# A one-core decoder layer with 32 experts: three gate_up widths, an order of the experts worked out on the chip, and changed stage openings

## The chip, the core and the metric

The kernel runs on one core of a Trainium2 chip. The metric is the device time of one launch in microseconds. The kernel before was timed three times: median 2191.45 us, from 2190.69 to 2195.38. Lower is better. The core has five engines with programs of their own, which meet only at semaphores: TensorE (PE, with its weight loads listed as PEld), VectorE (DVE), ScalarE (ACT), GpSimd (POOL) and SyncE (SP, which only issues DMAs here).

## The reference

One layer over x of 1024 tokens by 1024 features, all float32:

- h = RMSNorm(x); one projection h @ W_in of 3584 columns. 2048 of them feed four retention heads (rotary, chunks of 128, decay, norm, gate), 1536 feed eight stick-breaking attention heads of 64.
- x = x + concat(retention, attention) @ W_out.
- x = x + MoE(RMSNorm(x)): a router picks the top 4 of 32 experts per token with softmax weights over the four logits.

The mixture of experts, cut to its core:

```
top_logits, top_idx = lax.top_k(xf @ w_router + b_router, 4)
top_w = softmax(top_logits)
for each expert e, for its tokens xb:
    gu     = xb @ w_gate_up[e] + b_gate_up[e]      # 1024 -> 2048
    gate   = min(gu[:, 0::2], 7);  up = clip(gu[:, 1::2], -7, 7)
    hidden = (up + 1) * gate * sigmoid(1.702 * gate)
    y      = hidden @ w_down[e] + b_down[e]        # 1024 -> 1024
    out[token] += y * weight
```

There are 4096 assignments of a token to an expert, 128 per expert in the mean. Gate and up columns alternate in w_gate_up. An expert's weights are 12.6 MB.

## The kernel before

**Stages ahead of the experts (0 to 647 us).** Each tile of 128 tokens is normalised and transposed (`turn_tile`). The input projection goes in two halves of 512 tokens, 28 slabs of weights in all. Each float32 operand is split into an upper part (fp32r) by ACT and the rest by DVE (`upper_tokens`, `lower_tokens` and their like for slabs), and three products are summed (L946, L953). Of the first half's four tiles, DVE normalises 0 and 1 and POOL 2 and 3 (L592). Retention runs beside the projection. Then come the stick-breaking attention (393 to 508 us), the output projection (L1103 to L1105), the second norm and the router. Attention uses the difference `dv` of the values `sv` and the values shifted by one token: SP issues the shift as DMAs when the whole projection is done, POOL subtracts (L613).

**From the router to the first expert.** DVE picks the four best experts of each tile (`best`), PE ranks the tokens per expert (L1147, L1151), and DVE builds one-hot rows (`first_hot`), from which PE makes the list of expert 0's tokens. POOL gathers these rows from DRAM (`xn_scratch`, L616), PE transposes them (`turn_main`, `turn_over`), and DVE writes them as `xT`. Then `tables` on DVE (L1665 to L1679) builds the weights and places of all tokens, before the counters that PE waits for are raised (L1684). `keep_busy` is a row of transposes whose results nobody reads.

**The loop.** Every expert is one block, in the order 0 to 31, in a loop on all engines. In a block PE does:

- gate_up (L1246): 8 steps `f`, each 16 matmuls of 128x128 weights from `gu_ring` against w columns of `xT`. The weights of one matmul are every second column of a 256 wide piece (gate, then up). A branch on the expert's token count takes the program of w = 140 or w = 168, the most that a block holds. Step f writes PSUM bank f%2, which DVE must have emptied (`m_up`). After f = 3 comes `token_list` for the next expert (L1162).
- down (L1226): 48 matmuls for each half of the output with split operands; the next tokens' transposes lie inside. Tokens 129 to 160 go through `down_over(0)` and 161 to 168 through `down_over(1)`, 64 matmuls each (L1234), under a branch.

DVE adds biases, clips and multiplies per step, works out the next list (`list_hot` in f = 1, L1637 its first instruction, L1644 its largest; `list_out` in f = 4), and makes the lower parts of w_down. In block 0 it also does `table_part`, tables for experts over 168 tokens, which don't occur with these inputs. ACT does the sigmoid and the upper parts. SP asks for the next expert's weights as each quarter of `gu_ring` and the halves of `dn_ring` come free. POOL gathers the next tokens and adds this block's rows to the output in DRAM.

Semaphores count up over the whole run, and waits in the loop are on n times a constant. Nothing is planned at run time but the two branches.

## Time and profile before

One profiled execution took 2190.32 us, and its span, first to last instruction, is 2188.0 us.

| | |
|---|---|
| PE busy | 2126.4 us, 97% of the span |
| PE weight loads busy | 1891.9 us |
| DVE busy | 1271.9 us, 58% |
| ACT busy | 765.9 us, 35% |
| POOL busy | 346.5 us, 16% |
| chain of waits | PE 95%, DVE 2%, issue 1%, DMA 1% |
| moved by DMA | 509.53 MB |

Busy time is the union of an engine's instructions; weight loads lie beside matmuls. The chain of waits is followed back from the last instruction, at each step to what released it. "issue" is time in which an engine waited for nothing that the profile shows. A window's row gives the busy time of each engine in a stretch with the number of instructions in brackets, then the mean clock of PE as a share of full speed (PEclk), the DMA engines' share and their GB/s. A bare number such as 128x140 is the output of one instruction. L946 is line 946.

### The profile page before, as it was taken

Reading aid. Unit: us, or ns where it says so; the run is one execution under the profiler, and the core shown is the slowest. Engines: PE = TensorE matmul, PEld = TensorE weight load, DVE = VectorE, ACT = ScalarE, POOL = GpSimd, SP = SyncE. Lnnn points to the kernel's source line nnn. Section 1 sums busy time; section 2 is a strip of 40 time slices with the busy share of each in tenths; the row PEclk is TensorE's granted clock in tenths of the full one; section 3 lists DMA queues with packets and bytes.
Section 4 is the critical chain, followed back from the end, with each engine's and each line's share of the span. In section 5 each row is a group of like instructions: output and inputs, shape, how many; then the busy total and the mean of one; then the engine's idle time right before and its main releaser. Section 6 shows DMA issues by size and latency. Waiting matters only on the chain.

```text
span 2188.0 us, 41248 instructions
## 1 busy us (share of the span) xinstructions
PE 2126.4 (97%) x16059; PEld 1891.9 (86%) x16060; DVE 1271.9 (58%) x2564; ACT 765.9 (35%) x1369; POOL 346.5 (16%) x243
## 2 busy tenths in 40 slices
PE   7999999899979999999999999999999999999996
PEld 6887888677868999898899999899999999999996
DVE  6434534886466665456556655555666655666654
ACT  4143133666222333233333323333333332333332
POOL 3100200200011111111121111111212111212121
PEclk9999999999979999999999999999999999999998
DMA  5321221304366988788789888877998887999883
GB/s 179 105 79 58 97 96 39 116 1 154 126 209 220 323 307 293 238 279 307 274 298 318 306 293 280 307 270 263 320 325 307 306 294 264 319 327 331 309 290 89
DMA packets 253683, 509.53 MB, mean 233 GB/s; under 512 B 7466, under 2 KB 36318, under 8 KB 253342
## 3 DMA queue, kind: packets, MB, share of 16 engines
q1 hardware_dynamic: 230124, 451.95, 57.9%
q0 software_dynamic: 21968, 51.67, 9.6%
q10 hardware_dynamic: 1536, 5.15, 0.7%
q8 instruction: 38, 0.62, 0.1%
q14 instruction: 17, 0.14, 0.0%
HBM read 473.09 MB, written 33.55 MB: 232 GB/s over the span
## 4 chain that ended last, share of the span: by engine, by line
PE 95%; DVE 2%; issue 1%; DMA 1%; POOL 0%; ACT 0%; ACTq 0%; SPq 0%; DVEq 0%; POOLq 0%
PE bank L1246 46%; PE bank L1226 16%; PE bank L946 10%; PE bank L953 4%; PE bank L1234 3%; PE bank L1056 2%; PE bank L1069 2%; PE bank L1103 1%; PE bank L1169 1%; PE bank L1105 1%; PE bank L1104 1%; PE bank L1162 1%; PE bank L1040 1%; PE bank L1175 1%; PE bank L1211 1%
## 5 line engine op out<-in xcount | busy, mean ns | idle before, releaser
L1246 PE MATMUL bank<-hx,ring 128*128 128x140 f32 (+1 forms) x8192 | 1021.9, 287 | 7.5 <-DVEq L1684 7.5
L1246 PEld LDWEIGHTS bank<-hx,ring 128*128 128x128 f32 x8192 | 1015.1, 197 | 10.3 <-DVEq L1684 7.7
L1226 PE MATMUL bank<-work_r,hx_r 128*128 128x512 f32 x1024 | 335.0, 408 | 0.0
L1723 DVE TENSOR_TENSOR mix_r<-ring,work_r 128x1024 fp32r<-128x1024 f32 x256 | 305.0, 1223 | 41.1 <-ACT work_r L872 40.9
L889 ACT ACTIVATE hx<-hx 128x168 f32<-128x168 f32 x256 | 88.0, 344 | 595.8 <-DVE hx L1739 593.4
L1739 DVE TENSOR_SCALAR hx<-bank,small 128x168 f32<-128x168 f32 x256 | 100.3, 392 | 298.7 <-PE bank L1246 289.3
L872 ACT ACTIVATE work_r<-ring 128x1024 fp32r<-128x1024 f32 x256 | 257.7, 1042 | 0.0
L1226 PEld LDWEIGHTS bank<-work_r,hx_r 128*128 128x128 f32 x1024 | 188.1, 189 | 43.9 <-issue 10.4
L1226 PE MATMUL bank<-mix_r,hx_r 128*128 128x512 f32 x512 | 200.0, 391 | 0.0
L649 POOL DMA_INDIRECT out_x<-hx,small x32 | 52.0, 1625 | 659.7 <-ACT hx L882 621.3
L880 ACT ACTIVATE hx<-bank,small 128x512 f32<-128x512 f32 x64 | 44.0, 688 | 313.9 <-PE bank L1175 167.3
L616 POOL DMA_INDIRECT hx<-xn_scratch,small x33 | 33.9, 1028 | 574.1 <-issue 568.1
L895 ACT ACTIVATE hx_r<-hx 128x128 fp32r<-128x128 f32 x256 | 78.8, 308 | 109.0 <-DVE hx L1749 109.0
L946 PE MATMUL bank<-hx_r,mix_r 128*128 128x512 f32 x480 | 112.5, 392 | 3.6 <-DVE hx_r L1337 3.6
L1226 PEld LDWEIGHTS bank<-mix_r,hx_r 128*128 128x128 f32 x512 | 96.1, 188 | 21.0
L946 PE MATMUL bank<-hx_r,work_r 128*128 128x512 f32 x480 | 113.7, 394 | 0.0
L946 PEld LDWEIGHTS bank<-hx_r,mix_r 128*128 128x128 f32 x480 | 89.6, 188 | 23.5 <-issue 5.2
L1644 DVE TENSOR_TENSOR work<-hx,cst 128x3072 bf16<-128x3072 f32 x32 | 107.2, 3351 | 0.0
L946 PEld LDWEIGHTS bank<-hx_r,work_r 128*128 128x128 f32 x480 | 89.7, 188 | 20.2 <-issue 1.9
L652 POOL DMA_INDIRECT out_x<-hx,small x64 | 100.7, 1573 | 19.5 <-issue 19.5
L1741 DVE TENSOR_SCALAR hx<-bank,small 128x168 f32<-128x168 f32 x256 | 98.0, 383 | 0.0
L1658 DVE TENSOR_TENSOR hx<-bank,small 128x512 f32<-128x512 f32 x66 | 42.6, 686 | 86.0 <-PE bank L1169 86.0
(244 smaller groups left out, 2318.4 us busy)
## 6 DMA issues: line engine op xcount, KB each, us to landing
ring<-in_w_gate_up SPq DMA_DIRECT2D x128, 2048.0 KB, 11.0
ring<-in_w_down SPq DMA_DIRECT2D x64, 2048.0 KB, 17.5
mix<-in_w_in SPq DMA_DIRECT2D x14, 1024.0 KB, 5.0
work<-in_w_in SPq DMA_DIRECT2D x14, 1024.0 KB, 5.1
ring<-in_x SPq DMA_DIRECT2D x8, 512.0 KB, 6.3
hx<-in_w_out SPq DMA_DIRECT2D x1, 4096.0 KB, 14.0
work<-in_x ACTq DMA_DIRECT2D x8, 512.0 KB, 4.7
out_x<-work SPq DMA_DIRECT2D x8, 512.0 KB, 4.5
```

What stands on the lines that cost most here:

```text
L652: e.indirect_dma_start(out=out_quarters, in_=y_o[:, r], in_offset=None, compute_op=ALU.add, out_offset=bass.IndirectOffsetOnAxis(ap=idx_sc ...
L872: e.activation(dn_hi[:, nh, k:k + 2], dn_ring[:, k:k + 2, nh * CH:(nh + 1) * CH], ACT.Copy).then_inc(c_hi, 1)
L889: e.activation(sg[:, f % 2], g1[:, f % 2], ACT.Sigmoid, scale=GALPHA).then_inc(m_sig, 1)
L895: e.activation(hid_hi[:, f], hid[:, f, 0:P], ACT.Copy).then_inc(h_hi, 1)
L946: mm = e.matmul(dst, ws[b][:, k, u["s"] * P:(u["s"] + 1) * P], xs[:, k, :], start=k == 0 and (xs is x_hi and ws is w_hi), stop=k == KD - 1 ...
L953: mm = e.matmul(dst, xs[:, KD // 2 * b + k, u["s"] * P:(u["s"] + 1) * P], ws[b].rearrange("p (k a) n -> p k (a n)", a=2)[:, k, :], start=b ...
L1226: mm = e.matmul(bank[2 + t][:, :], h[:, k], w[:, t, k], start=False, stop=k == KD - 1 and w is dn_lo, skip_group_check=True)
L1246: mm = e.matmul(bank[f % 2][:, part * CAP:part * CAP + w], gu_ring[:, k, f * 256 + part:(f + 1) * 256:2], xT[:, k, 0:w], start=k == 0, sto ...
L1644: e.tensor_tensor(hot, pos_s.unsqueeze(2).to_broadcast([P, NT, NH * P]), slot_at.unsqueeze(1).to_broadcast([P, NT, NH * P]), ALU.is_equal) ...
L1723: e.tensor_tensor(dn_lo[:, nh, k:k + 2], dn_ring[:, k:k + 2, nh * CH:(nh + 1) * CH], dn_hi[:, nh, k:k + 2].bitcast(F32), ALU.subtract).the ...
L1739: e.tensor_scalar(g1[:, b], bank[b][:, 0:CAP], be[:, f:f + 1], GLIM, ALU.add, ALU.min)\
L1741: e.tensor_scalar(u1[:, b], bank[b][:, CAP:2 * CAP], be[:, 8 + f:9 + f], GLIM + 1.0, ALU.add, ALU.min).then_inc(m_up, 1)
```

## The change

1. *Widths and order.* There are three gate_up programs, 128, 140 and 168 columns wide (`WIDTHS`), chosen by two nested branches. Experts 0, 1 and 2 stay first (`FIXED`); of the others, those over 140 tokens (`LATER`) come last. The order is worked out on DVE during block 1 (`order_part`), so every engine that needs a block's expert (SP for its loads, DVE for its tables) reads it from `it_i` in memory. A new semaphore `it_go` says how many entries are ready; SP waits for it, and so does PE before its token count.
2. *Tables.* The opening's `tables` are split: the second expert's list (`second_lists`, `second_hot`) and the weights and places (`weight_table`, `place_table`) go into block 0, `order_part` into block 1 and `table_part` into block 2. ACT's split of b_down (`bias_part`) also moves into block 0.
3. *First tiles.* Tile 2 is normalised by ACT and tile 3 by DVE instead of POOL. PE does 14 idle transposes before the first vectors.
4. *Second token half.* Half of its split (`upper_tokens`, `lower_tokens`) is done before the last slab of the first half ends (g == NG // 2 - 3).
5. *Stick-breaking values.* `dv` is two regions; the first half's shift and subtraction are done within the projection.
6. *Output projection.* 20 idle transposes at its opening; `best` and `route_sum` of a tile are placed earlier in the loop over tiles.
7. *Experts' opening.* The rows of b_gate_up are loaded early into part of `dn_ring`, and their transposes stand earlier on PE; the second half of w_down waits for them. The last tile of normalised tokens is stored by ACT, not SP.

The diff, cut (only changed lines, indentation reduced):

```
@@ -58,9 +58,11 @@
-WIDTHS = (140, CAP)
-IT_STEPS = 17
-F_SPREAD = 20
+WIDTHS = (128, 140, CAP)
+LATER = (140,)
+FIXED = 3
+IT_STEPS = 28
+F_SPREAD = 21
...
-  b_rows = region(work, 4096, 2048)[0:NE]
+  b_rows = dn_ring[0:NE, 0:4, 512:1024]
...
@@ -530,6 +540,12 @@
+   def shifted(q):
+    lo = HT * q
+    for r0, r1 in ((1, 113), (113, P)):
+     e.dma_start(dv[q][r0:r1], sv[r0 - 1:r1 - 1, lo:lo + HT]).then_inc(z_shift[q], 16)
+    e.dma_start(dv[q][0:1, 1 - q:HT], sv[P - 1:P, lo - q:lo + HT - 1]).then_inc(z_shift[q], 16)
@@ -540,32 +556,35 @@
+    if j == NSLAB // 2 + 4:
+     e.wait_ge(prj_free, freed(NG // 2))
+     e.wait_ge(xs_lo, KD)
+     shifted(0)
-   for q in range(2):
-    lo, n = HT * q, HT - 1 + q
-    for r0, r1 in ((1, 113), (113, P)):
-     e.dma_start(dv[r0:r1, lo:lo + HT], sv[r0 - 1:r1 - 1, lo:lo + HT]).then_inc(z_shift[q], 16)
-    e.dma_start(dv[0:1, lo + 1 - q:lo + HT], sv[P - 1:P, lo - q:lo + HT - 1]).then_inc(z_shift[q], 16)
+   shifted(1)
-   for c in range(2):
-    e.dma_start(dn_ring[:, :, c * 512:(c + 1) * 512], dn_r[0, c]).then_inc(dn_in[c], 16)
+   e.dma_start(dn_ring[:, :, 0:512], dn_r[0, 0]).then_inc(dn_in[0], 16)
+   e.dma_start(b_rows, b_gate_up[0].rearrange("e (a n) -> e a n", n=512)).then_inc(bias_in, 16)
-    e.wait_ge(e_norm, i + 1)
-    e.dma_start(xnr[i], xn2[:, i % 2]).then_inc(e_st[i % 2], 16)
+    if i + 1 < NT:
+     e.wait_ge(e_norm, i + 1)
+     e.dma_start(xnr[i], xn2[:, i % 2]).then_inc(e_st[i % 2], 16)
+   e.wait_ge(bias_tr, 1)
+   e.dma_start(dn_ring[:, :, 512:1024], dn_r[0, 1]).then_inc(dn_in[1], 16)
@@ -576,7 +595,8 @@
-    load_expert(n, n)
+    e.wait_ge(it_go, n + 1)
+    load_expert(n, e.value_load(it_i[0:1, 0, bass.ds(n, 1)], min_val=0, max_val=NE - 1))
@@ -586,19 +606,25 @@
-   for i in range(2, HT):
-    e.wait_ge(a_inv, i + 1)
-    e.wait_ge(a_tr, 2 * i - 2)
-    e.tensor_scalar(x_norm[i % 2], x_in[i % HT], rstd[:, i:i + 1], None, ALU.mult).then_inc(a_norm_p, 1)
+   def differences(q):
+    for i in range(HT):
+     e.wait_ge(z_shift[q], 48)
+     e.tensor_tensor(dv[q][:, i], sv[:, HT * q + i], dv[q][:, i], ALU.subtract).then_inc(z_dv, 1)
+    if th:
+     e.wait_ge(xs_lo, KD)
+     e.memset(dv[0][0:1, 0], 0.0).then_inc(z_zero, 1)
+     e.wait_ge(z_zero, 1)
+     differences(0)
...
@@ -716,12 +738,15 @@
+   e.wait_ge(a_inv, 3)
+   e.wait_ge(a_tr, 2)
+   e.activation(x_norm[0], x_in[2], ACT.Copy, scale=rstd[:, 2:3]).then_inc(a_norm_2, 1)
-   upper_tokens(0)
+   upper_tokens(0, 0, KD)
-     upper_tokens(1)
+     upper_tokens(1, KD // 2, KD)
@@ -751,6 +776,8 @@
+    if g == NG // 2 - 3:
+     upper_tokens(1, 0, KD // 2)
@@ -833,36 +860,37 @@
+    if i == NT - 1:
+     logits_part(NT - 3)
-   for i in range(NT - 3, NT):
+   e.wait_ge(e_norm, NT)
+   e.dma_start(xnr[NT - 1], xn2[:, (NT - 1) % 2]).then_inc(e_last, 16)
+   for i in range(NT - 2, NT):
-   e.wait_ge(e_log, NT)
-   e.wait_ge(e_st[0], 128)
-   e.wait_ge(e_st[1], 128)
-   e.dma_start(b_rows, b_gate_up[0]).then_inc(bias_in, 16)
-   e.wait_ge(sc_done, 48)
-   e.wait_ge(f_step, F_SPREAD)
-   e.activation(bias_d, b_raw, ACT.Copy).then_inc(b_cast, 1)
...
+   def bias_part(g):
+    if g == 0:
+     e.wait_ge(sc_done, 48)
+     e.wait_ge(f_step, F_SPREAD)
+     e.activation(bias_d, b_raw, ACT.Copy).then_inc(b_cast, 1)
+    else:
+     e.wait_ge(b_sub, g)
+     for h in range(g, 3):
+      rows = slice(h * NE, (h + 1) * NE)
+      cp = e.activation(bias_d[rows], b_raw[rows], ACT.Copy)
+     cp.then_inc(b_cast, 1)
...
@@ -893,11 +921,14 @@
+     if opening and 1 <= f <= 3:
+      bias_part(f - 1)
-   with e.Fori(0, NE) as n:
+   block_act(0, opening=True)
+   with e.Fori(1, NE) as n:
@@ -924,6 +955,7 @@
+   keep_busy(14, bank[2])
...
@@ -1084,13 +1116,22 @@
+   keep_busy(20, bank[4])
+   def route_sum(i):
+    e.wait_ge(e_pev, i + 1)
+    if i:
+     e.wait_ge(e_logb, 6 * i - 5)
+    e.matmul(bank[7][:, 0:NE], l_part[:, i % 2], cst[:, C_SEL:C_SEL + NE], start=True, stop=True).then_inc(e_log, 1)
+     if nh and i >= 3:
+      route_sum(i - 3)
@@ -1126,12 +1167,6 @@
...
-    if 3 <= i:
+    if NT <= i:
@@ -1154,7 +1189,13 @@
-   keep_busy(10, bank[4])
+   e.wait_ge(bias_in, 16)
+   e.wait_ge(e_x2, 16)
+   for j in range(16):
+    mm = e.transpose(bank[j // 8][:, (j % 8) * NE:(j % 8 + 1) * NE],
+        b_rows[:, j % 8 // 2, j % 2 * 256 + j // 8:j % 2 * 256 + 256:2], cst[0:NE, C_ID:C_ID + NE])
+   mm.then_inc(bias_tr, 1)
@@ -1187,19 +1228,14 @@
...
+   keep_busy(10, bank[4])
-   keep_busy(8, bank[3])
+   keep_busy(4, bank[3])
@@ -1292,6 +1328,7 @@
+    e.wait_ge(it_go, n + 1)
...
@@ -1352,9 +1389,11 @@
-   for i in range(HT):
+   to_raw(0)
+   normalise(3)
+   for i in range(1, HT):
-   lower_tokens(0)
+   lower_tokens(0, 0, KD)
...
@@ -1440,6 +1479,8 @@
+    if g == NG // 2 - 3:
+     lower_tokens(1, 0, KD // 2)
@@ -1550,13 +1591,15 @@
+    if 3 <= i < NT:
+     best(i - 3)
-    if 3 <= i:
+    if NT <= i:
@@ -1601,30 +1644,52 @@
-   step(e.tensor_tensor(f_w0, f_a[:, :, :, 0], f_w, ALU.mult))
-   step(e.tensor_reduce(f_t0, f_w0, X, ALU.add))
-   step(e.tensor_copy(tw_s[:, :, 2], f_t0))
-   step(e.tensor_tensor(f_t0, f_t0, tw_s[:, :, 2], ALU.subtract))
-   step(e.tensor_copy(tw_s[:, :, 3], f_t0))
-   step(e.tensor_tensor(f_t0, f_t0, tw_s[:, :, 3], ALU.subtract))
-   e.tensor_copy(tw_s[:, :, 4], f_t0).then_inc(l_hot, 1)
+   step(e.tensor_tensor(f_w0, f_a[:, :, :, 0:2], f_w.unsqueeze(3).to_broadcast([P, NT, 4, 2]), ALU.mult))
+   step(e.tensor_reduce(f_t0, f_w0.rearrange("p i k e -> p i e k"), X, ALU.add))
+   def weight_parts(x_e):
+    w = f_t0[:, :, x_e]
+    step(e.tensor_copy(tw_s[:, :, 2], w))
+    step(e.tensor_tensor(w, w, tw_s[:, :, 2], ALU.subtract))
+    step(e.tensor_copy(tw_s[:, :, 3], w))
+    step(e.tensor_tensor(w, w, tw_s[:, :, 3], ALU.subtract))
+    return e.tensor_copy(tw_s[:, :, 4], w)
+   weight_parts(0).then_inc(l_hot, 1)
+   step(e.tensor_copy(it_i[:, 0, 0:NE], iota_e))
+   e.sem_inc(it_go, FIXED)
-   step(e.tensor_reduce(f_t, f_b.rearrange("p i k e -> p i e k"), X, ALU.add))
-   def tables():
-    e.memset(it_base, 0.0)
-    e.memset(it_low, 0.0)
+   def second_lists():
+    step(e.tensor_scalar(pos_t, tok_id, f_cnt[:, 1:2], None, ALU.add))
+    step(e.scalar_tensor_tensor(pos_t, rank[:, :, 1], -2.0, pos_t, ALU.mult, ALU.add))
+    step(e.tensor_tensor(pos_t, pos_t, f_n[:, :, 1], ALU.mult))
+    step(e.tensor_tensor(pos_s, rank[:, :, 1], pos_t, ALU.add))
+    step(weight_parts(1))
+    step(e.tensor_reduce(f_t, f_b.rearrange("p i k e -> p i e k"), X, ALU.add))
+   def second_hot():
+    e.tensor_tensor(hot, pos_s.unsqueeze(2).to_broadcast([P, NT, NH * P]),
+        slot_at.unsqueeze(1).to_broadcast([P, NT, NH * P]), ALU.is_equal).then_inc(l_hot, 1)
+    e.sem_inc(l_wrap, 1)
+    e.sem_inc(l_pos, 1)
+   def weight_table():
+   def place_table():
+    e.memset(it_base, 0.0)
+    e.memset(it_low, 0.0)
...
+   square = [P, NE, NE]
+   def order_part(f):
+    if f == 0:
+     table(e.tensor_copy(c_f, it_i[:, 1, 0:NE]))
+     table(e.tensor_scalar(c_class, c_f, float(LATER[0]), None, ALU.is_gt))
+     for w in LATER[1:]:
+      table(e.scalar_tensor_tensor(c_class, c_f, float(w), c_class, ALU.is_gt, ALU.add))
+     table(e.scalar_tensor_tensor(c_class, iota_e, float(FIXED), c_class, ALU.is_ge, ALU.mult))
+     table(e.scalar_tensor_tensor(c_key, c_class, float(NE), iota_e, ALU.mult, ALU.add))
+    elif f == 2:
+     table(e.tensor_tensor(c_less, c_key.unsqueeze(2).to_broadcast(square),
+          c_key.unsqueeze(1).to_broadcast(square), ALU.is_gt))
+     table(e.tensor_reduce(c_rank, c_less, X, ALU.add))
+    elif f == 3:
+     table(e.tensor_tensor(c_at, iota_e.unsqueeze(2).to_broadcast(square),
+          c_rank.unsqueeze(1).to_broadcast(square), ALU.is_equal))
+    elif f == 4:
+     table(e.tensor_tensor(c_less, c_at, iota_e.unsqueeze(1).to_broadcast(square), ALU.mult))
+     table(e.tensor_reduce(it_f[:, 0, 0:NE], c_less, X, ALU.add))
+    elif f == 5:
+     table(e.tensor_tensor(c_less, c_at, c_f.unsqueeze(1).to_broadcast(square), ALU.mult))
+    elif f == 6:
+     table(e.tensor_reduce(it_f[:, 1, 0:NE], c_less, X, ALU.add))
+     table(e.tensor_copy(it_i[:, :, FIXED:NE], it_f[:, :, FIXED:NE]))
+     e.sem_inc(it_go, NE - FIXED)
@@ -1727,11 +1816,13 @@
-   def block_dve(n, x_e, x_next=None, opening=False):
+   def block_dve(n, x_e, x_next=None, opening=False, ordering=False, tabling=False):
+    if opening:
+     second_lists()
@@ -1748,12 +1839,21 @@
-     if f == 1:
+     if f == 1 and opening:
+      second_hot()
+     elif f == 1:
-       x_next = e.value_load(it_i[0:1, 0, bass.ds(n + 1, 1)], min_val=0, max_val=NE)
+       x_next = e.value_load(it_i[0:1, 0, n + 1:n + 2] if isinstance(n, int) else
+            it_i[0:1, 0, bass.ds(n + 1, 1)], min_val=0, max_val=NE)
-     if opening:
+     if opening and f == 0:
+      weight_table()
+     if opening and f == 2:
+      place_table()
+     if ordering:
+      order_part(f)
+     if tabling:
@@ -1777,11 +1877,12 @@
-   block_dve(0, 0, 1, True)
-   assert built[0] == IT_STEPS
-   with e.Fori(1, NE - 1) as n:
-    block_dve(n, n, n + 1)
-   block_dve(NE - 1, NE - 1)
+   block_dve(0, 0, 1, opening=True)
+   block_dve(1, 1, 2, ordering=True)
+   block_dve(2, 2, tabling=True)
+   assert built[0] == IT_STEPS, built[0]
+   with e.Fori(FIXED, NE) as n:
+    block_dve(n, e.value_load(it_i[0:1, 0, bass.ds(n, 1)], min_val=0, max_val=NE - 1))
```

## Rows read from the trace of the kernel before

**Rows 1.** Timeline of PE: start us, us, what; in brackets idle before and releaser.
```profile
206.82 3.46 PE L946 MATMUL bank<-hx_r,mix_r 128*128 128x512 f32 x14 [2.56 <-DVE hx_r L1337]
...
393.65 0.70 PE L1069 MATMUL bank<-work,ring 128*64 128x128 f32 x4 [4.07 <-POOL ring L613]
...
511.51 0.47 PE L1103 MATMUL bank<-ring_r 128*128 128x512 f32 x1 [3.36 <-DVE hx_r L1548]
...
647.24 1.07 PE L1246 MATMUL bank<-hx,ring 128*128 128x140 f32 x3 [7.47 <-DVEq L1684]
```

**Rows 2.** Windows, one a block: us, PE, PEld, DVE, ACT, POOL, PEclk, DMA, GB/s.
```profile
647.24:700.90 53.66, 50.87 (x416) 46.24 (x417) 36.15 (x82) 14.36 (x27) 3.54 (x3) 0.95 0.52 178
793.33:841.27 47.94, 47.94 (x417) 43.62 (x416) 28.57 (x64) 15.82 (x29) 8.41 (x6) 1.00 0.86 295
841.27:898.62 57.35, 57.35 (x480) 51.47 (x480) 28.58 (x64) 15.83 (x29) 7.85 (x6) 1.00 0.72 247
1281.03:1334.93 53.90, 53.90 (x416) 49.53 (x416) 28.57 (x64) 15.81 (x29) 7.84 (x6) 1.00 0.78 263
1529.13:1573.57 44.44, 44.44 (x352) 41.71 (x352) 28.59 (x64) 15.83 (x29) 8.40 (x6) 1.00 0.93 319
```

**Rows 3.** Lines by form, whole span: busy us, mean ns of one, idle before.
```profile
L1234 PE MATMUL bank<-ring,hx 128*32 128x256 f32 x1216 | 68.8, 379 | 0.0
```

**Rows 4.** Timeline of PE: retention's short matmuls, and a block's first two pieces.
```profile
158.38 1.06 PE L992 MATMUL bank<-ring,work 128*128 128x128 f32 x8
...
160.17 0.60 PE L1015 MATMUL bank<-cst,ring 128*128 128x128 f32 x4
...
1900.96 15.42 PE L1246 MATMUL bank<-hx,ring 128*128 128x140 f32 x128
1916.21 0.75 PE L1162 MATMUL bank<-hx,work 128*128 128x5 bf16 x24
```

**Rows 5.** One line's weight loads: ns of one (least, median, most), when.
```profile
L1226 PEld LDWEIGHTS bank<-work_r,hx_r x1: 186/186/186, 1617.0 to 1617.0; 128*128 128x128 f32 x1
...
L1246 PEld LDWEIGHTS bank<-hx,ring x1: 194/194/194, 1916.8 to 1916.8; 128*128 128x128 f32 x1
```

**Rows 6.** Windows: the end of a block of 44.4 us.
```profile
1987.42:1988.92 1.50, 1.50 (x15) 0.92 (x13) 0.23 (x2) 0.12 (x1) 0.00 (x0) 1.00 0.00 0
```

**Rows 7.** Timeline of DVE and PE, last block (it starts at 2126.84).
```profile
2136.72 0.23 DVE L1637 TENSOR_SCALAR small<-hx 128x8 f32 x1 [0.72 <-issue]
...
2141.93 0.75 PE L1162 MATMUL bank<-hx,work 128*128 128x5 bf16 x24
```

**Rows 8.** Chain of waits, start of the program: start us, us, what.
```profile
13.64 2.84 POOL ring L592
...
22.22 5.74 PE bank L946 x24
```

**Rows 9.** Windows: PE after the waits at 393.65 and 511.51.
```profile
393.00:400.00 7.00, 6.35 (x34) 4.48 (x34) 3.45 (x3) 1.79 (x5) 7.00 (x7) 0.53 0.93 325
512.00:516.00 4.00, 3.88 (x11) 2.74 (x11) 4.00 (x7) 4.00 (x9) 0.00 (x0) 0.57 1.03 410
```

**Rows 10.** Chain of waits: the gather, and a stall in block 0.
```profile
626.64 7.89 DMA hx<-xn_scratch,small
...
681.12 2.79 issue
```

**Rows 11.** Lines by form, DVE, 618 to 700 us: a pass of 1024 elements.
```profile
L1612 DVE TENSOR_TENSOR work<-cst,work 128x1024 f32<-128x1024 bf16 x1 | 1.2, 1226 | 0.0
```

**Rows 12.** Windows: the stages ahead of the router's end.
```profile
55.00:601.60 546.60, 533.42 (x3200) 428.64 (x3199) 285.12 (x354) 227.07 (x392) 48.35 (x29) 0.99 0.26 87
```

**Rows 13.** Instruction queues: packets, MB, share; 55 to 601.6, 660 to 702, 702 to 2169.
```profile
q8 instruction: 26, 0.43, 0.3%
...
q8 instruction: 6, 0.10, 0.9%
...
q14 instruction: 2, 0.02, 0.0%
```

More of the change, by code:

```diff
@@ L487, in layer @@
         f_s = region(work, 1568, NT)
-        f_w0 = region(work, 1576, NT, 4)
-        f_t0 = region(work, 1608, NT)
+        f_w0 = region(work, 1576, NT, 4, 2)
+        f_t0 = region(work, 1640, NT, 2)
         f_cnt = region(mix, 7744, NE)
+        c_f = small[:, 898:898 + NE]
+        c_rank = small[:, 898 + NE:898 + 2 * NE]
+        c_key = small[:, 898 + 2 * NE:898 + 3 * NE]
+        c_class = small[:, 898 + 3 * NE:898 + 4 * NE]
+        c_less = region(mix, 6144, NE, NE)
+        c_at = region(mix, 7168, NE, NE)
         f_over = region(mix, 7776, NE)
@@ L608, in _ @@
             e.wait_ge(prj_free, freed(NG))
-            e.memset(dv[0:1, 0], 0.0).then_inc(z_zero, 1)
-            e.wait_ge(z_zero, 1)
-            for i in range(NT):
-                e.wait_ge(z_shift[i // HT], 48)
-                e.tensor_tensor(dv[:, i], sv[:, i], dv[:, i], ALU.subtract).then_inc(z_dv, 1)
+            differences(1)
             def gather_main(landed):
@@ L703, in upper_slab, with upper_tokens @@
                 e.activation(w_hi[j % 2], w_raw[j % 2], ACT.Copy).then_inc(ws_hi, 1)
-            def upper_tokens(th):
+            def upper_tokens(th, first, last):
                 e.wait_ge(a_hx, NT * (th + 1))
                 if th:
-                    e.wait_ge(prj, NG // 2)
-                for k in range(0, KD, 2):
+                    e.wait_ge(prj, end_of[NSLAB // 2 - 2] if first == 0 else NG // 2)
+                for k in range(first, last, 2):
                     e.activation(x_hi[:, k:k + 2], x_raw[:, k:k + 2], ACT.Copy).then_inc(xs_hi, 1)
@@ L855, in _ @@
                 .then_inc(bias_ok, 1)
-            e.wait_ge(sc_done, 48)
-            e.wait_ge(f_step, F_SPREAD)
-            e.activation(bias_d, b_raw, ACT.Copy).then_inc(b_cast, 1)
-            for g in range(1, 3):
-                e.wait_ge(b_sub, g)
-                for h in range(g, 3):
-                    rows = slice(h * NE, (h + 1) * NE)
-                    cp = e.activation(bias_d[rows], b_raw[rows], ACT.Copy)
-                cp.then_inc(b_cast, 1)
+            def bias_part(g):
[9 more added lines that the diff above has]
+                    cp.then_inc(b_cast, 1)
             def upper(n, q):
@@ L883, in weigh_rows, with block_act @@
                                  scale=w_sc[:, 1 + r:2 + r]).then_inc(m_yo, 1)
-            def block_act(n):
+            def block_act(n, opening=False):
                 for f in range(KD):
@@ L1068, in values @@
                         h = units[m]["h"]
-                        mm = e.matmul(out_bank(u)[pr, cols], dv[:, u["k0"] // P + t, h * HD:(h + 1) * HD],
+                        mm = e.matmul(out_bank(u)[pr, cols], dv[u["k0"] // CH][:, t, h * HD:(h + 1) * HD],
                                       massT[m % 4][:, t * P:(t + 1) * P], start=u["diag"] and t == 0,
@@ L1127, in route @@
                 mm.then_inc(e_part, 1)
-            def route_sum(i):
-                e.wait_ge(e_pev, i + 1)
-                if i:
-                    e.wait_ge(e_logb, 6 * i - 5)
-                e.matmul(bank[7][:, 0:NE], l_part[:, i % 2], cst[:, C_SEL:C_SEL + NE], start=True, stop=True).then_inc(e_log, 1)
             for i in range(NT + 3):
@@ L1189, in _ @@
             mm.then_inc(p_list, 1)
-            e.wait_ge(bias_in, 16)
-            e.wait_ge(e_x2, 16)
-            for j in range(16):
-                mm = e.transpose(bank[j // 8][:, (j % 8) * NE:(j % 8 + 1) * NE],
-                                 b_rows[:, (j % 8) * 256 + j // 8:(j % 8) * 256 + 256:2], cst[0:NE, C_ID:C_ID + NE])
-            mm.then_inc(bias_tr, 1)
+            keep_busy(10, bank[4])
             e.wait_ge(l_hot, 1)
@@ L1332, in lower_slab, with lower_tokens @@
                 e.tensor_tensor(w_lo[j % 2], w_raw[j % 2], w_hi[j % 2].bitcast(F32), ALU.subtract).then_inc(ws_lo, 1)
-            def lower_tokens(th):
-                for q in range(KD // 2):
+            def lower_tokens(th, first, last):
+                for q in range(first // 2, last // 2):
                     e.wait_ge(xs_hi, KD // 2 * th + q + 1)
@@ L1681, in _ @@
                 tokens_out(m)
-            tables()
             for s_ in (m_up, m_gs, m_hid, m_dn):
```

26 lines of the change are left out of this document (13 added, 13 removed).

## The prediction

> **What bounds the kernel now.** The chain of waits is TensorE (PE) for 95% of the span, so I read where PE stands still, then the busy times block by block. PE stands still at the openings of stages [rows 1]: 2.56 us at 206.82, 4.07 at 393.65, 3.36 at 511.51, 7.47 at 647.24, where the first gate_up starts. From there expert blocks fill the span. A block has one of four lengths [rows 2]: 44.44 us, 47.94, 53.90, 57.35. PE is busy for the whole of each, at clock 1.00. Steps between them: 3.5 us is one down_over of 64 matmuls (an expert over 128 tokens), 5.95 us the 168 wide gate_up instead of the 140 wide (over 140). The 1216 matmuls of L1234 are 19 such steps [rows 3]; five experts are over 140 (one of them over 160, two steps), so 18 experts are over 128 and 14 are not. Those 14 are all that a 128 wide program can shorten.
>
> **The 128 wide program.** One L1246 instruction of 140 columns comes every (15.42 - 0.28)/127 = 119.2 ns (0.28 is the last one's own run) [rows 4]. [...] From a short matmul into the stretch the first strided load takes 194 ns, the first adjacent one 186 [rows 5]: 8 ns more. [...] 14 blocks x 256 x 1.1 ns = -4 us; ends 0 and -36. [...]
>
> **What the shorter block could run into.** The DMA engines are idle for some 3 us of a 44.45 us block ([rows 6]: share 0.00 near its end) and move 0.93 x 44.4 = 41.3 us of work. A block at the far end is 44.4 - 2.6 = 41.9, still above. Loading a block's expert from memory adds a register load to VectorE (DVE) and SP. DVE's at the block's start lies in its 2.5 us of waiting for PE. The one in f=1 is in the trace, in the last block: the list starts 0.72 us later, and the token list on PE comes at 2141.93, 15.09 us into its block [rows 7], as without it (1916.21 - 1900.96 = 15.25, [rows 4]). Cost 0. Putting five experts last changes no sum of PE.
>
> **Openings.** *Start.* Two normalisations go from POOL, where the second has 2.84 us on the chain [rows 8], to ACT and DVE; DVE needs 0.75 for such a tile. The last turn then starts some 2 us earlier; 14 added transposes before the first vectors may hold those back by 0.7 and lift the clock. -2.3 (0 to -3.5).
> *Second half of tokens.* Half of x is split before the last slab ends, so the 12 matmuls that don't need the rest (24 take 5.74, [rows 8], so 2.8 us) cover the wait of 2.56 [rows 1]. Next is slab 15, wanted at 215 instead of 217.7; ACT has it split at 211.2. -2.5 (0 to -2.56).
> *Stick breaking.* The difference of sv waits for a DMA and POOL at 393.65; its first half is made in the projections. The wait of 4.07 goes, and PE ran at clock 0.53 from 393 to 400 [rows 9], where 6.35 us of work is 3.4 at full clock; DVE and ACT bound the next stretch, so I count 1.0 of it. -5.1 (-2 to -7.5).
> *Output projection.* The wait of 3.36 stays (ACT and DVE split the first parts), 20 transposes fill it. The clock of 0.57 in 512 to 516 [rows 9] costs 0.43 x 3.88 = 1.7; DVE's 0.61 us per part lies just below PE's 0.68, so -1.3 (0 to -2).
> *Experts.* (a) best() ahead of residual, routing part 5 earlier: the chain of four best() of 1.6 us starts 1.4 earlier. (b) The bias rows no longer load in front of the gathers, and SP no longer waits for the last normalised tile before the first gate_up loads. Those 4 MB hold the gather at 7.89 us [rows 10]; they end 3 us earlier and the gather is issued 1.4 earlier, so it lands near 630 instead of 634.5. (c) The tables of DVE, 639.45 to 647.1, leave the opening. Tokens would be ready near 635. What is late next: PE must load the token count, branch over the new program, and wait for its code (below): 637. -10.2 (-7.5 to -13). (d) Block 0 shows clock 0.95 [rows 2], 0.05 x 53.66 = 2.7 us; PE no longer stands idle ahead of it: -2.0 (0 to -2.7).
>
> **What it adds to the first blocks.** A pass of 1024 elements on DVE costs 1.23 us (L1612, [rows 11]), and PE needs bank f%2 back within two steps of 3.83 us. Block 0 gets the second lists, weights and places (4.5, 4.0, 3.4 us) on DVE's 28.6: walked step by step, PE waits near f=4, 5 and 6, +2.5. Block 1 gets the order: seven such passes and small steps, 10.5 us, the most at f=4. DVE falls behind to 5 us at f=6; PE waits 2.2 at f=7 and 1.5 for the last hidden part, +3.7. Block 2 gets the tables of the old block 0, which hid there only behind the 2.79 us below: +1.2. Together +7.4 (0 to +13).
> *Added waits.* SP waits for the bias transposes ahead of the second half of w_down; all loads of expert 1 are queued behind it, wanted from block 0's f=1 on, and PE has the transposes some 12 us before. SP and PE wait for the order: three experts are free before block 0, the rest in block 1, and expert 3's loads are asked for in block 2. ACT issues the last store of normalised tokens; behind it stand the last logits, and POOL waits for its landing ahead of b_down and the gathers: beside the gate_up loads that may take 6 us instead of 3, still ahead of the gather. 0 for all.
>
> **Code of the loop.** PE issues 3200+3199 instructions from 55 to 601.6 us [rows 12] while its instruction queue q8 brings 26 pieces of 16 KB [rows 13]: some 250 each. From 660 to 702 it brings six, one of them at the 2.79 us stall of 681.12 ([rows 10], a branch over the program not taken), and from 702 to 2169 none: of the instruction queues only q14 stands there [rows 13]. The loop's code, two programs of 560 and 396 for down plus waits, about 1570 instructions or 6.3 pieces, is kept. With the third it is 2150 or 8.4 pieces. Blocks that take the 128 and 140 programs use only 1570 of them, as now. So I expect only first visits to cost: the 128 program in block 1, the 168 one near block 27, up to 2.79 each: +3 (0 to +8).
>
> **Sum.** -2.3 - 2.5 - 5.1 - 1.3 - 10.2 - 2.0 + 7.4 - 4 + 3 = -17.0. The profiled execution took 2190.3 (span 2188.0 and 2.3 around it), so 2173.3; the median shown is 1.1 higher: **2174 us**. Its own range is 2158 to 2188.
>
> **Rivals.**
> *The 128 program pays in full.* [...] For: nothing shows a strided load at 128 columns. Against: the 8 ns [rows 5]. 2174 + 4 - 31 = 2147 us. Chance 0.20. [...]
> *The code no longer stays.* The loop spans nine or ten pieces. If eight is what is kept (all that the trace shows kept), blocks that alternate between the 128 and 140 programs throw out each other's code, and the code is fetched behind weight loads that keep DMA at 0.93 [rows 2]. One exposed fetch of 2.79 in each of 28 blocks is +78: 2252 us. It decides from six blocks on: 6 x 2.79 eats the 17. Against: the code of a 140 or 128 block without the 168 program is no longer than today's. Chance 0.17. [...]
> *A wash.* DVE's new work in blocks 0 to 2 costs 13 instead of 7.4, the loads of 4 MB still hold the gather, and the early clock doesn't come: -17 + 5.6 + 5 + 5 = -1.4, 2190 us. For: DVE alone decides when bank f%2 comes free. Against: the 7.47 us is gone in any order. Chance 0.08.
>
> **Numbers.** Forecast 0.55. The range 2140 to 2192 takes in forecast, full gain and wash; it leaves out the code rival. 0.2% is 4 us, about what this measurement can tell from nothing. Faster by more: 0.55 + 0.20 + a third of the wash, less a little for my own upper end, 0.77. Within: 0.04. Slower: 0.19.
>
> **What would show it.** L1246 at 128 columns every 118 ns (right), 109 to 112 (first rival). Blocks of at most 128 tokens at 44.1 us, the over-140 ones as the last five at 53.9 and 57.4. First gate_up near 626 (11 us of earlier gains and 10 of its own). q8 silent in the loop but for the first visits; if it shows dozens of pieces with "issue" gaps at the branches, the second rival holds. Block 1 several us over its neighbours, DVE busy at 1.0 there. The forecast is wrong if the gaps at 206, 393 and 647 don't shrink, or if blocks after the third grow.

## The result: 15.8% slower, and the profile after

The changed kernel takes 2539.28 us (median of 4, 2533.82 to 2543.57) against 2192.06 for the one before: ratio 1.158 [1.155, 1.161]. The forecast was 2174, the range up to 2192. All times are medians; one execution of e2 below (3645.43 us at a mean granted clock of 0.557, where its other seven took 2188.64 to 2192.61) stands apart, and nothing here explains it. From the page of the changed kernel:

```profile
span 2531.8 us, 41674 instructions
...
PE 2197.3 (87%) x16089; PEld 1943.0 (77%) x16090; DVE 1282.4 (51%) x2582; ACT 726.7 (29%) x1339; POOL 343.1 (14%) x241
...
PEclk9999999998898889889888989989999999988888
...
q8 instruction: 210, 3.44, 0.6%
...
PE 80%; issue 10%; DVE 6%; ACT 2%; DMA 1%; ACTq 0%; POOL 0%; DVEq 0%; POOLq 0%
```

The instruction queue q8 brought 210 pieces (3.44 MB, so 16.4 KB each) where it brought 38 (0.62 MB) in the kernel before, and "issue" has 10% of the chain (1% before). I take q8 for the queue of PE's code, since one of its pieces is under way in every wait of the next rows. 178 of the 210 pieces belong to the 32 blocks (below). The waits of PE over the blocks, 635 to 2515 us (engine, line waited for: us in total, times, longest):

```profile
PE bank L1282 <- issue: 170.3, 19, 18.6
PE bank L1262 <- issue: 63.2, 12, 5.6
PE bank L1247 <- issue: 53.3, 13, 4.4
```

Together these are 286.8 us. I read them as waits for code, because of these pieces: L1282 is gate_up, L1247 is down's first matmul and L1262 the next ones. PE is busy 67.3 us longer than in e1 below (2197.3 against 2130.0), since the clock is lower behind the gaps: 0.925 in the mean, and 0.990 in e1. The two make 354.1; the spans of the two kernels differ by 353.7. Here is one block, an expert of the 140 program after another of it (timeline of PE):

```profile
1256.52 18.16 PE L1282 MATMUL bank<-hx,ring 128*128 128x140 f32 x128 [11.11 <-issue]
1275.12 15.51 PE L1282 MATMUL bank<-hx,ring 128*128 128x140 f32 x128
1294.79 0.61 PE L1247 MATMUL bank<-cst,small 96*128 96x512 bf16 x1 [4.16 <-issue]
1301.01 1.01 PE L1262 MATMUL bank<-work_r,hx_r 128*128 128x512 f32 x2 [5.61 <-issue]
1331.20 2.23 PE L1282 MATMUL bank<-hx,ring 128*128 128x140 f32 x8 [11.01 <-issue]
```

PE stops where it jumps over the 168 program to down (4.16, and 5.61 just behind it; q8 brings one piece during each), and where it jumps back and over the 128 program (11.01). 128 matmuls then take 18.16 us instead of 15.42 [rows 4]. The windows of three kinds of block, in the columns of [rows 2]: 140 after 140, 128 after 128, 168 after 168:

```profile
1256.52:1331.20 74.68, 53.90 (x414) 48.13 (x415) 28.63 (x64) 14.53 (x28) 8.46 (x6) 0.82 0.58 191
1823.06:1867.15 44.09, 44.09 (x351) 41.35 (x350) 28.58 (x64) 14.53 (x28) 8.43 (x6) 1.00 0.94 321
2308.00:2383.08 75.08, 56.73 (x415) 52.02 (x415) 28.67 (x64) 14.54 (x28) 7.95 (x6) 0.86 0.58 191
```

q8 brought 10 pieces in the first and in the last, none in the second. Three start from 1319 us on, around the single stall of 11.01 us that ends at 1331.20. The DMA queues of the first window, of 1319 to 1332 us, and of the blocks from 635 to 2515 us:

```profile
q8 instruction: 10, 0.16, 0.9%
...
q8 instruction: 3, 0.05, 1.7%
...
q8 instruction: 178, 2.92, 0.7%
```

So programs that alternate are not the cause: a 140 block behind a 140 block fetches everything anew, and so does 168 behind 168. Only in runs of the 128 program does the code stay.

The openings of stages, to be compared with [rows 1] (timeline of PE):

```profile
19.53 12.73 PE L978 MATMUL bank<-hx_r,mix_r 128*128 128x512 f32 x48 [3.42 <-DVE hx_r L1374]
...
206.23 5.96 PE L978 MATMUL bank<-hx_r,mix_r 128*128 128x512 f32 x25 [0.39 <-DVE hx_r L1374]
...
505.40 0.47 PE L1144 MATMUL bank<-ring_r 128*128 128x512 f32 x1 [1.03 <-DVE hx_r L1589]
...
634.99 18.31 PE L1282 MATMUL bank<-hx,ring 128*128 128x140 f32 x128 [5.86 <-issue]
```

2.56, 4.07 and 3.36 became 0.39, none and 1.03. The first gate_up starts 12.25 us earlier. The wait of 7.47 us ahead of it has become one of 5.86, now for code: q8 brings a piece at 631.9 us, within it, and e1 below has no wait there.

### The profile page after: what moved, and what is told of

It reads as the page before. It is cut to its first block, busy times and chain, and to the rows that moved or that the text cites. A ratio compares the mean times of both kernels' runs of the same rounds, so it can differ in the third digit from the quotient of the medians.

```text
span 2531.8 us, 41674 instructions
## 1 busy us (share of the span) xinstructions
PE 2197.3 (87%) x16089; PEld 1943.0 (77%) x16090; DVE 1282.4 (51%) x2582; ACT 726.7 (29%) x1339; POOL 343.1 (14%) x241
## 3 DMA queue, kind: packets, MB, share of 16 engines
q8 instruction: 210, 3.44, 0.6%
## 4 chain that ended last, share of the span: by engine, by line
PE 80%; issue 10%; DVE 6%; ACT 2%; DMA 1%; ACTq 0%; POOL 0%; DVEq 0%; POOLq 0%
PE bank L1282 39%; PE bank L1262 15%; PE bank L978 8%; PE bank L985 3%; PE bank L1270 3%; DVE mix_r L1812 2%; PE bank L1101 1%; PE bank L1088 1%; PE bank L1144 1%; PE bank L1210 1%; PE bank L1146 1%; PE bank L1145 1%; ACT work_r L900 1%; PE bank L1203 1%; PE bank L1072 1%
## 5 line engine op out<-in xcount | busy, mean ns | idle before, releaser
L1282 PE MATMUL bank<-hx,ring 128*128 128x128 f32 (+2 forms) x8192 | 1060.0, 293 | 171.7 <-issue 170.3
L1282 PEld LDWEIGHTS bank<-hx,ring 128*128 128x128 f32 x8192 | 1049.6, 203 | 181.3 <-issue 178.3
L1262 PE MATMUL bank<-work_r,hx_r 128*128 128x512 f32 x1024 | 350.4, 425 | 68.9 <-issue 63.2
L1262 PEld LDWEIGHTS bank<-work_r,hx_r 128*128 128x128 f32 x1024 | 199.7, 200 | 119.2 <-issue 80.1
L1262 PE MATMUL bank<-mix_r,hx_r 128*128 128x512 f32 x512 | 208.8, 408 | 0.0
L1262 PEld LDWEIGHTS bank<-mix_r,hx_r 128*128 128x128 f32 x512 | 101.5, 198 | 23.6
```

What stands on the lines that cost most here:

```text
L1262: mm = e.matmul(bank[2 + t][:, :], h[:, k], w[:, t, k], start=False, stop=k == KD - 1 and w is dn_lo, skip_group_check=True)
L1282: mm = e.matmul(bank[f % 2][:, part * CAP:part * CAP + w], gu_ring[:, k, f * 256 + part:(f + 1) * 256:2], xT[:, k, 0:w], start=k == 0, sto ...
```

## The experiments

Three theories. *Window*: PE keeps a fixed number of pieces of 16 KB; entering one also brings the next. I count a piece as 256 instructions, an estimate: [rows 12, 13] have 3200 matmuls and 3199 weight loads for 26 pieces, 246 each, without waits and branches. A block that visits more than are kept fetches all of them, every time. *Size*: what counts is the number of instructions in the loop, with a bound of 2048, my estimate from eight such pieces. *Alternation*: programs throw each other out when they change. Positions below are counted in the compiled PE program. Each ratio is against the kernel before timed beside that run (medians 2191.03 to 2192.48 us), with its 95% interval where it is given.

**e1: two programs in the changed kernel**

```
-WIDTHS = (128, 140, CAP)
+WIDTHS = (140, CAP)
```

> The changed kernel with WIDTHS back to (140, 168); order, openings and the rest stay. Both theories have the third program as the cause of the loss. Window theory (PE keeps eight pieces of 16 KB of code, and a piece that is entered brings the next along): the loop spans seven pieces, so q8 is silent in it, blocks after the third take 44.4, 47.9, 53.9 or 57.4 us as before. Size theory (a loop of up to 2048 instructions is kept): the same. The first gate_up starts at 632 to 635 instead of 647.2, blocks 0 to 2 give back 2 to 7 us: 2178 to 2186 us. If the order or the loads by a register cost anything in the loop, it is over 2200.

2177.76 us (5 runs), ratio 0.9934 [0.992, 0.9947]: a gain of 14.7. q8 brought 6 pieces in block 0 and then none until the last block. Windows of e1 (a block of 128 or fewer tokens, one over 140, and blocks 0 to 2):

```profile
1573.80:1618.25 44.45, 44.45 (x352) 41.71 (x351) 28.62 (x64) 14.54 (x28) 8.48 (x6) 1.00 0.94 318
1945.80:1999.72 53.92, 53.92 (x416) 49.44 (x414) 28.67 (x64) 14.52 (x28) 7.95 (x6) 1.00 0.78 263
632.59:686.85 54.26, 50.22 (x415) 44.75 (x415) 37.37 (x83) 17.94 (x30) 9.55 (x5) 0.97 0.76 276
686.85:733.27 46.42, 45.20 (x352) 41.74 (x351) 36.52 (x76) 14.47 (x28) 7.86 (x6) 1.00 0.89 305
733.27:783.15 49.88, 48.77 (x415) 43.53 (x414) 36.03 (x80) 14.47 (x28) 8.63 (x6) 1.00 0.83 284
```

So the third program costs 361.5 us (2539.28 - 2177.76). The order, the register loads and the openings are all still in e1, so they are not the cause.

**e2: eight more idle transposes ahead of the loop of the kernel before**

```
-keep_busy(8, bank[3])
+keep_busy(16, bank[3])
```

> The kernel before, its two programs untouched, with 16 transposes instead of 8 in the last idle row ahead of the loop: 16 instructions (8 matmuls, 8 weight loads) more, about 1 us of work. Window theory: the loop then starts at the very end of one 16 KB piece and ends at the start of another, eight pieces instead of seven and one brought along, nine where eight are kept: about 240 pieces on q8, some 26 blocks with two stalls each (one at the jump over the program not taken, one at the jump back) and 13 to 20 us longer, blocks over 140 tokens that follow one another spared: 2550 to 2750 us. Size theory and alternation theory: nothing happens but the 1 us, 2193 us.

2191.43 us, ratio 0.9992 [0.9981, 1.0002]: the window theory's forecast failed. Either it was wrong, or I had the position of the code wrong.

**e3: the three programs in reverse order in the code**

```
-half = len(widths) // 2
-with e.If(tokens <= widths[half - 1]):
-    choose(widths[:half])
+with e.If(tokens > widths[-2]):
+    gate_up(n, widths[-1])
 with e.Else():
-    choose(widths[half:])
+    choose(widths[:-1])
```

> The changed kernel with its three programs in the other order in the code: 168 first, then 140, then 128, same sizes, same order of the experts. Window theory: now the run of the five experts over 140 is the one that stays (53.9 to 57.4 us each, no pieces but at its start), and every block of 128 or 140 fetches ten pieces, with 44.1 us blocks of the long run of small experts becoming 62 to 71: about 270 pieces, 2800 to 2920 us. Alternation theory (programs throw each other out only when they change): runs of one class stay wherever the program stands, so the seven small blocks in a row stay at 44.1 us and the time is near 2540.

2767.01 us, below the 2800 to 2920 that I had named; the count of pieces in the loop (about 270 forecast, 273 came) and the clean run of over-140 blocks came as named. Windows of e3, a 128 block in its long run and a 168 one in its run:

```profile
2092.81:2155.94 63.13, 45.76 (x351) 42.66 (x351) 28.58 (x64) 14.54 (x28) 8.45 (x6) 0.85 0.70 228
2583.29:2637.18 53.89, 53.89 (x416) 49.54 (x415) 28.65 (x64) 14.53 (x28) 7.94 (x6) 1.00 0.77 263
```

q8 brought 10 pieces in the first and none in the second. Roles are swapped, as the window theory says. Alternation falls: seven small blocks in a row pay every time. The count of instructions falls as the full account: the same 2140 cost 228 us more than in the changed kernel when they stand in another order.

**e4: the third program alone, in the kernel before**

```
-WIDTHS = (140, CAP)
+WIDTHS = (128, 140, CAP)
```

> The kernel before with WIDTHS (128, 140, 168) and nothing else: experts in their natural order, old openings. Window theory: the loop starts some 60 instructions lower in its piece than in the changed kernel, so that even blocks of the 128 program touch nine pieces: about 212 pieces, 53 stalls at a mean 7.4 us (350 us over 47 in the changed kernel), 2190 + 390 = 2580, 2530 to 2650 us, and no run of clean 44.1 us blocks anywhere. Alternation theory: the same classes in a row (blocks 25 to 29, all at most 128) run at 44.1 us, about 2550.

2496.77 us, ratio 1.1389. The third program costs some 300 us without anything else of the change. But the time came below my range, and small blocks in a row (26 to 29) ran clean, that is without a fetch, at 44.1 us, where I had expected none. The positions were off again.

I refitted the number kept and the offset of the code to the pieces of each block in six traces; nine fitted best.

**e5 and e6: a loop of 1950 instructions, at two positions**

```
-                    with e.If(tokens > P + OV):
-                        down_over(1)
...
+                kd = KD - 1 if w == CAP else KD
...
-keep_busy(8, bank[3])
+keep_busy(20, bank[3])     # e5; 76 in e6
```

> The shift had no effect, so the bound of eight pieces was wrong. Refitted to the piece counts of all blocks of the six traces so far: nine pieces of 256 instructions stay, and a piece that is entered brings the next along. Test: the changed kernel with all three programs, the loop cut from some 2140 to some 1950 PE instructions. Left out: tokens 161 to 168 of an expert in down (down_over(1)), and the last eighth of the contraction in the 168 program. 12 more idle transposes ahead of the loop put its start early in a piece: eight pieces spanned and one brought along. Window theory: only first visits, about 10 pieces on q8 from 634 us on, blocks of 44.1, 47.9 and (five last, less work) 49.4 us: 2145 to 2160 us. The count of instructions alone (under 2048) says the same. A theory by which a third program, or nested branches, cost by themselves: over 2400.

> The same loop, instruction by instruction, behind 68 idle transposes more than the changed kernel has instead of 12 (112 instructions, some 6 us). The loop now lies over nine pieces and brings a tenth along. Window theory: about 130 pieces and 32 stalls at 8 us, in blocks of the 140 program and at the change to the 128 one, 60 to 75 us each, while the run of seven small blocks and the five last stay clean: 2380 to 2440 us. Count of instructions alone: 2157 us, as the kernel beside it plus 6.

2408.47 and 2422.02 us. e5 missed its forecast by some 250 us. It refutes "nine are kept", and with it the count of instructions as a bound of 2048: with 1950 in the loop, a 140 block behind another one still fetches nine pieces. e6 came into its range, but by luck: some 167 pieces came in the loop where I had expected 130, and its five last blocks took 65 to 70 us and weren't clean.

**e7: experts sorted in three classes**

```
-LATER = (140,)
+LATER = (128, 140)
```

> The changed kernel with LATER = (128, 140): experts of at most 128 tokens, then 129 to 140, then the rest, so that the program changes 5 times in the run instead of 16. Window theory: it doesn't help, since a block of the 140 or the 168 program alone visits ten pieces: 12 clean blocks of 44.1 us, then eleven of 72 to 75 and five of 73 to 76, about 176 pieces and 50 stalls: 2540 to 2600 us. Alternation theory: about 2190 us.

2580.00 us, within its range. Twelve blocks run at 44.10, then all of the others at 71 to 81. (The changed kernel changes its program 14 times, not 16; this one 5 times.) Sorting more makes it worse than the changed kernel. The number of pieces is the same (210 in both), but PE waits 38 us longer for them: 140 blocks in a row pay the long wait at the jump back every time (9.9 to 11.1 us in the run of them).

With the nine traces of the kernels before, after and e1 to e7 the fit has one answer: eight pieces are kept, one more is brought along, and the code lies 35 to 40 instructions later in its pieces than I had counted. A kept set of 7, 9 or 10 misses several of the kernels altogether. Whether the piece fetched longest ago or the one used longest ago goes first, these traces don't tell. This is what the fit gives: first and last instruction of the loop, in pieces, and the pieces that a block of each program visits or brings along. e9 and e10 were still to run:

```
kernel            loop from-to    visited + brought along   fetched in the loop
before            30.00-36.13     7 + 1                     first visits only
e2                30.07-36.19     7 + 1                     first visits only
e1                30.24-36.36     7 + 1                     first visits only
after, e7         30.24-38.61     140, 168: 10; 128: 8      yes; none in runs of 128
e3                30.24-38.61     128, 140: 10; 168: 8      yes; none in runs of 168
e4                30.00-38.37     140, 168: 10; 128: 8      yes; none in runs of 128
e5                30.33-37.94     140, 168: 9; 128: 7       yes; none in runs of 128
e6                30.77-38.38     140, 168: 9; 128: 8       yes; none in runs of 128
e9                29.96-36.08     128, 140: 9; 168: 8       yes; one or none in 168
e10               30.24-36.60     7 + 1                     first visits only
```

The 128 program in the changed kernel visits 30 to 32 and 36 to 38 and brings 33 and 39: eight, so it stays. And the kernel before begins within five instructions of a boundary. e2 had moved it the harmless way, further into the piece.

**e9: the kernel before with twelve instructions less**

```
-keep_busy(8, bank[3])
+keep_busy(2, bank[3])
```

> The cut kernel still fetched, so the bound was refitted to all nine traces: eight pieces of 256 instructions are kept after all (first in, first out), a piece that is entered brings the next along, and PE's code lies 35 to 40 instructions later in its pieces than I took. Then the kernel before begins its loop in the first five instructions of a piece and spans seven, and the shift of e2 went the harmless way. Test: the kernel before with 2 instead of 8 transposes in the last idle row ahead of the loop (12 instructions less, nothing else). The loop begins at the end of a piece: eight visited and one brought along, nine where eight are kept. Window theory: nine pieces in each of the 27 blocks of at most 140 tokens, about 241 in all, two stalls a block (4 and 10 us as in e5), 62 to 66 us instead of 44 to 48, while the five blocks over 140 stay at 53.9 and 57.3 with none: 2640 to 2680 us. Counts of instructions, alternation, or noise of the alignment: 2191 us.

2659.76 us, ratio 1.2133 [1.211, 1.216]. In a kernel that is otherwise the one before, with both its programs, 21% are lost. The pieces of q8 from 647.55 to 2638 us (DMA queues), then a small block and one over 140 (windows):

```profile
q8 instruction: 241, 3.95, 0.9%
```

```profile
2457.47:2522.23 64.76, 48.65 (x351) 45.01 (x350) 28.57 (x64) 15.81 (x29) 8.41 (x6) 0.87 0.65 219
960.16:1014.06 53.90, 53.90 (x415) 49.54 (x414) 28.57 (x64) 15.82 (x29) 7.85 (x6) 1.00 0.77 263
```

The time was named ahead within the range, and the count as about 241. That it came out to the piece is luck: some small blocks fetch 8 and not 9, and the five blocks over 140 tokens are spared, but not wholly. One has no piece; four have one each and take 1.8 to 2.6 us more than before.

**e10: three programs in seven pieces**

```
-                    with e.If(tokens > P + OV):
-                        down_over(1)
...
+                kd = 2 if w == CAP else KD
```

> The changed kernel with all three programs in a loop of some 1630 instructions that spans seven pieces. Left out: tokens 161 to 168 of an expert in down, and six of the eight k steps of the 168 program. Window theory: q8 silent after the first visits (about 40 pieces in all), 44.1 us and 47.9 us blocks however the classes alternate, and the last five bounded by their weights' transfer at 40 to 45 us: 2100 to 2130 us. If three programs or the nested branch cost by themselves: still over 2350.

2097.61 us, just under the range, because four of the short last blocks took 38 to 40 us where I had expected 40 to 45. The time is below all others because this kernel leaves work out. From 700 us on q8 brought two pieces, both in the last block. Windows of e10, the 128 and the 140 program, which still alternate 13 times:

```profile
1570.72:1614.82 44.10, 44.10 (x351) 41.35 (x350) 28.57 (x64) 14.53 (x28) 8.45 (x6) 1.00 0.94 321
1062.58:1110.51 47.93, 47.93 (x416) 43.61 (x415) 28.61 (x64) 14.53 (x28) 8.46 (x6) 1.00 0.86 295
```

44.10 us is 44.09 in the changed kernel, 47.93 is 47.94 in [rows 2]: three programs and nested branches cost nothing where the code stays.

**e8, e11 and e12: the version that is left**

e8 is e1 with 139 instead of 140 columns, e11 is e8 without the order, e12 has 30 idle transposes instead of 14 ahead of the first projection.

```
-WIDTHS = (140, CAP)
+WIDTHS = (139, CAP)
...
-                    table(e.tensor_scalar(c_class, c_f, float(LATER[0]), None, ALU.is_gt))
...
-                    table(e.tensor_copy(it_i[:, :, FIXED:NE], it_f[:, :, FIXED:NE]))
...
-            keep_busy(14, bank[2])
+            keep_busy(30, bank[2])
```

> e1 with WIDTHS (139, 168). [...] So 139 columns come every 118.3 to 118.4 ns, 0.8 less than 119.2, in 27 blocks of 256: 5.8 us less than e1's 2177.8, 2172. If the load sets the pace at 140 columns already (the step from 128 to 140 is not linear), nothing, 2178.

2174.60 us, ratio 0.9924 [0.991, 0.9937]; 2172 was forecast. A small block takes 44.28 us (e1: 44.45). That is 27 x 0.17 = 4.6 us of the 5.8 forecast; the medians give 3.2. The 0.8 ns of a column in the forecast had been shown for wider ones only: from 140 to 168 columns it is (53.90 - 47.94)/(28 x 256) = 0.83 ns [rows 2]. This run has 0.85: (15.31 - 0.28)/127 = 118.35 ns, after 119.2.

> e8 (two programs, 139 and 168 wide, the new openings) without the order: experts in their natural order, order_part cut to the one copy that table_part needs. Block 1 gives back the 1.9 us that DVE's order costs there; all else stays: 2172.5 us, 2171 to 2174. If interleaved classes cost anything with two programs, it is slower than e8's 2174.6.

2171.85 us, ratio 0.9904 [0.9887, 0.992]. Block 1 takes 44.42 us, and 46.33 in e8: the 1.9 us of the order are back.

> e11 with 30 instead of 14 idle transposes between the last turned tile and the first projection. In e8 PE stands idle 3.35 us there and the 48 matmuls behind take 14.0 us, 11.2 in the kernel before, which is the part of the start that I had counted wrong. With the gap filled they take 11.2 to 12: 1.5 to 2.8 us less at the second turn, the rest of the run the same: 2170 to 2172. If the clock falls there whatever PE does, nothing changes.

2170.87 us, ratio 0.9903 [0.9886, 0.9919]. The rows of the first 48 matmuls, e11 and then e12:

```profile
20.38 12.75 PE L978 MATMUL bank<-hx_r,mix_r 128*128 128x512 f32 x48 [2.87 <-DVE hx_r L1374]
```

```profile
19.77 11.14 PE L978 MATMUL bank<-hx_r,mix_r 128*128 128x512 f32 x48 [1.96 <-DVE hx_r L1374]
```

The 1.6 us are there in the trace, and so is the reason: over the 48 matmuls the granted clock is 0.87 in e11 and 1.00 in e12, from 22 to 24 us 0.50 and 1.00. At the gather's first transposes e12 is still 1.7 us ahead (625.57 against 627.25), but from there to the first gate_up its clock is 0.54 where e11 has 0.81, and it starts only 0.3 us ahead. The medians differ by 1.0. e11 and e12 are the fastest that compute everything: e12 is 20.6 us (0.9%) under the kernel before and 14.5% under the changed one.

## Why the prediction was wrong

The failed step is "Code of the loop": "Blocks that take the 128 and 140 programs use only 1570 of them, as now. So I expect only first visits to cost", +3. It came to +366: 361.5 for the third program, plus the 4.9 that the 128 width saves within it. I had counted instructions executed. What counts, by the fit, is pieces visited and brought along, and a block of the 140 program has ten (as q8 brought from 1256.52 to 1331.20): the loop's head and the one behind it, its own three and the one behind, three for down and the one behind. The second rival had the right mechanism ("if eight is what is kept", chance 0.17), but a wrong price and a wrong condition. It assumed one fetch of 2.79 us in each of 28 blocks (+78). The trace of the changed kernel has 44 waits for code, 19 ahead of a gate_up and 25 at the start of down, up to 18.6 us each, and the clock falls behind them (0.82 and 0.86 over a block). Nor is it the change between two programs that costs, by the 140 blocks in a row of e7.

The rows to see it were there. [rows 13] show six pieces in the first block and none behind it; the loop of 1570 instructions (6.1 pieces of 256; the prediction says 6.3) lies over seven, and with the one brought along eight were all that the trace showed kept. The 8.4 pieces of the new loop were over it. I let the number of instructions used stand against that, which no row supported. In straight code the pieces cost little: 26 come in 546.6 us, of which PE is busy 533.42, so they cost 13.2 us at most [rows 12, 13]. The 44 waits here, 286.8 us, lie at taken jumps or just behind them.

The other steps can be read from e1, where the blocks are undisturbed, and from the openings of the changed kernel. A step's gain is what the trace has gained on the kernel before at the step's end, less what it had at the step's start. The changed kernel and e1 run the same code up to the first gate_up, and their traces still differ by up to 2.8 us there (505.40 and 508.22), so a term of 1 or 2 us is not settled by one trace:

- 128 wide program, -4: right. 44.10 us a block where e1 has 44.45, 14 x 0.35 = -4.9. No run shows the 1.1 ns in this term, an estimate: 128 matmuls take 15.23 us in the block at 1823.06, (15.23 - 0.28)/127 = 117.7 ns, 1.5 less than 119.2. The first rival (109 to 112) is out, and the 31 us of its sum are shown by no run. Its far end, 10.0 ns an instruction, is what 12 columns come to at the 0.83 ns that a column costs between 140 and 168 (e8 above). Below 140 the step shrinks: in e8 139 columns come every 118.35 ns (15.31 us for 128), so from there to 128 it is 0.06 ns a column. What holds 128 columns at 117.7 ns isn't shown. Retention's matmuls of that size come every 111.9 (16 in the 1.79 us from 158.38 to 160.17, [rows 4]), with weights of adjacent columns; no run has the gate_up matmul with such weights.
- Start, -2.3: half right. The first projection begins 2.7 us earlier, but behind 3.42 us of idle its 48 matmuls take 12.73 us and not 11.16, and -1.1 is left at the second turn (32.91 for 34.02; e1 -1.2). The cause is the clock, 0.87 over these matmuls and 1.00 in the kernel before; e12, with less idle ahead of them, keeps it at 1.00.
- Second half of tokens, -2.5: came to -1.6 (382.56 for 385.29 at the end of the stage, less the 1.1 above), and in e1 to -0.1 (384.05). The wait at 206 did shrink, to 0.39.
- Stick breaking, -5.1: came to -3.4 (505.40 for 511.51 at the output projection's first matmul, less 2.7), and in e1 to -2.0 (508.22). The wait of 4.07 has gone; new ones of 2.11 and 0.52 on DVE's L1512 stand a few us later.
- Output projection, -1.3: right, -1.7 (608.51 for 616.32 at the last tile's router matmuls, less 6.1), and -1.7 in e1 too (611.35).
- Experts' opening, -10.2: right, -9.7 in e1 (632.59 for 647.24, less the 5.0 of e1 at the point above). Nearly all of it is the tables' part: from the gathered tokens' first transposes to the first gate_up it is 4.15 us for 12.66. The transposes themselves start at 628.44 for 634.58, 6.1 us earlier of which 5.0 are gains ahead of the stage, so the gather gave 1.2 of the 4.5 forecast.
- Clock and DVE's work in blocks 0 to 2, -2.0 + 7.4 = +5.4: +4.5 (783.15 - 632.59 = 150.6 for 146.1). Block 2 pays more of it (49.88 us for 47.93, +1.9 where 1.2 was forecast) and block 1 less (46.42 for 44.50, +1.9 where 3.7 was forecast).

Without the code term the sum was -20.0, of which -16.0 without the 128 program. e1's terms add up to -10.2 (-1.2 - 0.1 - 2.0 - 1.7 - 9.7 + 4.5), and its profiled execution is 10.4 us under that of the kernel before (2179.90 for 2190.32). The medians say -14.7: the profiled execution of e1 is the slowest of its five. So that the median comes near -16.0 is partly luck. By the traces a third of the forecast gain did not come, above all in stick breaking, the second half of tokens and the start.

## What to carry to other kernels

Count the code of a hot loop on TensorE by position, in the pieces that q8 brings (16.4 KB each here). In all kernels here, a block behind one of the same program ran without a fetch where the pieces that its path visits, plus those brought along, were eight at most, and paid where they were nine or ten. A loop near that bound is best padded ahead so that it starts early in a piece (the kernel before, 2191.48 us, against e9, 2659.76), and looked at again after any edit ahead of it: q8 has to be silent within the loop. The total of pieces alone doesn't give the price (210 in both e7 and the changed kernel, at 2580.00 and 2539.28 us). A third copy of a program that saves 0.35 us in each of 14 blocks is to be weighed against that first; one program made a column narrower gave about as much, 0.17 us in each of 27.
